# State space output projection: column parts with the norm done part by part, chunks normed six tiles ahead, gates kept in device memory

## The reference, cut to what matters

```python
def _ssd_mixer(h, in_w, conv_w, conv_b, dt_bias, A_log, D_skip, norm_g, out_w):
    ...                                     # z, xs, Bm, Cm, dt from h @ in_w, convolved
    y = _ssd_chunked(xs * dt[..., None], dt * A, Bm, Cm)
    y = y + (xs * D_skip[:, None]).reshape(bsz, L, SSD_D_INNER)
    y = y * jax.nn.silu(z.astype(jnp.float32))
    yg = y.reshape(bsz, L, SSD_N_GROUPS, -1)                       # 8 groups of 512 columns
    yg = yg * lax.rsqrt(jnp.mean(jnp.square(yg), -1, keepdims=True) + RMS_EPS)
    y = yg.reshape(bsz, L, SSD_D_INNER).astype(h.dtype) * norm_g
    return y @ out_w                                               # 256 x 4096 @ 4096 x 2048

x = _layer_norm(DEEPNORM_ALPHA * x + (1.0 + gate) * y, ln_g[layer], ln_b[layer])
if layer == N_A_LAYERS - 1:
    k_sh, v_sh = _shared_kv(x, kv_w)
```

## Time and profile before

| | |
|---|---|
| median of three runs | 3442.06 us |
| profiled execution | 3440.7 us, span 3439.0 us |
| PE busy | 3259.9 us (95%) |
| PEld busy | 2977.3 us (87%) |
| DVE busy | 2384.2 us (69%) |
| ACT busy | 1609.5 us (47%) |
| POOL busy | 677.1 us (20%) |
| chain that ended last | PE 82%, DVE 6%, issue 4%, ACT 3%, PEld 2%, POOL 2%, DMA 1% |
| transfers | 665.63 MB, mean 194 GB/s |

### The profile page before, as it was taken

The page is one execution under the profiler, slowest core; times in us unless marked ns, Lnnn a source line. Parts: engine busy times, 40 slices in busy tenths (PEclk is TensorE's granted clock), DMA queues, the critical chain, the costliest instruction groups (busy, mean ns, idle before and its releaser), DMA issues.

```text
span 3439.0 us, 64842 instructions
## 1 busy us (share of the span) xinstructions
PE 3259.9 (95%) x21994; PEld 2977.3 (87%) x21994; DVE 2384.2 (69%) x3811; ACT 1609.5 (47%) x2252; POOL 677.1 (20%) x636
## 2 busy tenths in 40 slices
PE   7989999999999999999999989999998969999997
PEld 7787899999889998899777879998887859987995
DVE  6665469189778987899898776335777876554455
ACT  4654445533453345433344555445665444444442
POOL 1000029800111001100000116884222111100001
PEclk9999999999999999999999999999999989999998
DMA  6434545666786668766556864656665767765443
GB/s 194 148 98 147 162 147 156 184 203 212 238 264 216 212 219 263 245 209 212 165 172 184 266 210 147 185 188 195 210 207 180 265 210 229 246 192 174 138 129 123
DMA packets 185323, 665.63 MB, mean 194 GB/s; under 512 B 24112, under 2 KB 24320, under 8 KB 184304
## 3 DMA queue, kind: packets, MB, share of 16 engines
q1 hardware_dynamic: 149696, 545.89, 50.0%
q0 software_dynamic: 35504, 118.08, 11.3%
HBM read 661.71 MB, written 2.16 MB: 193 GB/s over the span
## 4 chain that ended last, share of the span: by engine, by line
PE 82%; DVE 6%; issue 4%; ACT 3%; PEld 2%; POOL 2%; DMA 1%; DVEq 0%; SPq 0%; POOLq 0%; PEldq 0%; ACTq 0%
PE PS L564 14%; PE PS L565 14%; PE PS L566 14%; PE PS L914 7%; PE PS L916 6%; PE PS L918 6%; PE PS L635 2%; PE PS L636 2%; PE PS L637 2%; POOL w_lo L465 2%; PE PS L656 2%; PE PS L660 2%; PE PS L658 2%; PE PS L866 1%; ACT w_hi L1259 1%
## 5 line engine op out<-in xcount | busy, mean ns | idle before, releaser
L1259 ACT ACTIVATE w_hi<-raw 128x1024 fp32r<-128x1024 f32 x1032 | 1093.8, 1061 | 1634.5 <-PE PS L566 934.9
L1799 DVE TENSOR_TENSOR w_lo<-raw,w_hi 128x1024 fp32r<-128x1024 f32 x872 | 1072.9, 1233 | 674.1 <-ACT w_hi L1259 668.0
L564 PE MATMUL PS<-xt_hi,w_hi 128*128 128x256 f32 x4608 | 1332.2, 289 | 22.8 <-POOL w_lo L465 7.3
L565 PE MATMUL PS<-xt_lo,w_hi 128*128 128x256 f32 x4608 | 1311.8, 285 | 0.0
L566 PE MATMUL PS<-xt_hi,w_lo 128*128 128x256 f32 x4608 | 1311.1, 285 | 0.0
L564 PEld LDWEIGHTS PS<-xt_hi,w_hi 128*128 128x128 f32 x4608 | 892.5, 194 | 34.6 <-issue 24.2
L565 PEld LDWEIGHTS PS<-xt_lo,w_hi 128*128 128x128 f32 x4608 | 892.6, 194 | 0.4
L566 PEld LDWEIGHTS PS<-xt_hi,w_lo 128*128 128x128 f32 x4608 | 892.0, 194 | 0.0
L465 POOL TENSOR_TENSOR w_lo<-raw,w_hi 128x1024 fp32r<-128x1024 f32 x160 | 405.0, 2540 | 223.0 <-ACT w_hi L1259 222.1
L914 PE MATMUL PS<-w_hi,st_hi 128*128 128x512 f32 x1024 | 403.7, 394 | 1.5 <-issue 1.3
L916 PE MATMUL PS<-w_hi,st_lo 128*128 128x512 f32 x1024 | 400.6, 391 | 0.0
(11 more groups left out here) (381 smaller groups left out, 3571.7 us busy)
## 6 DMA issues: line engine op xcount, KB each, us to landing
raw<-in_u_emb SPq DMA_DIRECT2D x256, 512.0 KB, 3.6
raw<-in_v_emb SPq DMA_DIRECT2D x256, 512.0 KB, 4.3
ada<-in_ada_w POOLq DMA_DIRECT2D x240, 256.0 KB, 4.5
raw<-in_xbc SPq DMA_DIRECT2D x96, 512.0 KB, 3.5
raw<-in_z SPq DMA_DIRECT2D x80, 512.0 KB, 3.6
raw<-in_q SPq DMA_DIRECT2D x64, 512.0 KB, 3.5
raw<-in_a_out SPq DMA_DIRECT2D x64, 512.0 KB, 4.9
raw<-in_k SPq DMA_DIRECT2D x48, 512.0 KB, 4.1
```

Source lines behind the costliest of these rows:

```text
L564: pe.matmul(o, w_h, x_h, start=start, stop=False, skip_group_check=True)
L565: pe.matmul(o, w_h, x_l, start=False, stop=False, skip_group_check=True)
L1259: act.activation(w_hi[:, u, :], raw[:, u, :], ACT.Copy).then_inc(hi_done, 1)
L1799: dve.tensor_tensor(w_lo[:, u, :], raw[:, u, :], w_hi[:, u, :].bitcast(F32), ALU.subtract)\
```

## The change

In the z stage the sums of squares are taken from PSUM by DVE, scaled and inverted at once (`inverted_sum`, at the last head of each group), and ACT takes the root of four groups in one instruction, at head 57 and again at a_out's tile 4. The banks of z and of these sums are other ones.

The projection is unrolled. `norm_tile(i)` does the first 1024 columns of chunk i in tiles 0 to 31 (banks 0 to 3), then 512 columns of two chunks a tile: tiles 32 to 47 into banks 4 and 5, tiles 48 to 63 into banks 6 and 7. The host stores the weights in that order. All chunks keep their high and low parts in `a_hi` and `a_lo`. DVE norms chunk i + 6 and makes the low part of chunk i + 3 at step i. When a part is done, DVE multiplies by the gate row, adds X and takes bn_stats of its columns; parts 0 and 1 do that at steps 33 to 38 and 49 to 54, the last one behind tile 63.

PE transposes the gate (`turn_gates`), ACT copies it, POOL stores it to device memory (`gates_kept`) and reads it back to all partitions as `a_gate` and, before b_out, `gate_row`. The diagonals and their matmuls are gone.

X is normed by mean and root in pieces of 512 columns, half of the tokens on ACT and half on DVE, between the steps of the split that follows PE's transposes. Gain and bias go into that split as scale and bias of each partition (`balanced`, which the xbc stage had before as a written out loop); X itself gets them in `rows_applied`, inside k2 behind its bodies 3 and 6.

```diff
@@ PE
+            def norm_tile(i):
+                pe.wait_ge(lo_done, 4 * FIRST_BODY["a_out"] + i + 1)
+                if i < XC:
+                    pieces = [(i, g * 512, 2 * tt + g, tt) for tt in range(TT) for g in range(2)]
+                else:
+                    part, pair = divmod(i - XC, XC // 2)
+                    pieces = [(2 * pair + k, k * 512, 4 + 2 * part + tt, tt) for k in range(2) for tt in range(TT)]
+                pe.wait_ge(stage_lo_done, CHUNKS["a_out"] + pieces[-1][0] + 1)
...
-            all_rows("a_out", (first_banks, other_banks))
-            gate_rows(0)
-            pe.wait_ge(sem("x4_done"), 1)
+            pe.wait_ge(sem("cb_done"), SG)
+            pe.wait_ge(sem("xd_done"), 2 * SG)
+            pe.wait_ge(sem("sums_out"), SG - 1)
+            for i in range(4 * NB["a_out"]):
+                if i == XC:
+                    pe.wait_ge(sem("z_taken"), XC)
+                    pe.wait_ge(sem("sums_out"), SG)
+                if i == XC + XC // 2:
+                    pe.wait_ge(sem("y_added"), XC)
+                    pe.wait_ge(sem("gates_out"), 1)
+                norm_tile(i)
+                if i == 1:
+                    pe.wait_ge(sem("y_added"), XC - 1)
+                    group_sum(SG - 1, 5)
+                    pe.wait_ge(sem("z_taken"), XC - 1)
+                    ada_sum("z", 3, ada_acc_z)
+                if i == 6:
+                    turn_gates()
             turn(3)
@@ PE, turn
+                    if n == 3 and c % 4 == 0:
+                        pe.wait_ge(sem("x_normed"), c // 4 + 1)
+                        pe.wait_ge(sem("x_normed_too"), c // 4 + 1)
@@ POOL
             pool.wait_ge(sem("sums_out"), SG)
-            pool.wait_ge(sem("gates_split"), 1)
-            norm_operands(0)
-            with pool.Fori(0, 16) as k:
+            ada_tiles("a_out", 0, ada_a)
+            pool.wait_ge(sem("gates_out"), 1)
+            pool.dma_start(gates_kept.rearrange("n (c p) -> c n p", p=P), gate_t[:, :, :]).then_inc(sem("gates_stored"), 16)
+            pool.wait_ge(sem("gates_stored"), 16)
+            pool.dma_start(a_gate[:, :], gates_kept[0].partition_broadcast(P)).then_inc(sem("gate_loaded"), 16)
+            with pool.Fori(1, 16) as k:
                 ada_tiles("a_out", k, ada_a)
-            norm_rows(0)
@@ ACT, a_out
+            for i in range(4 * NB["a_out"]):
+                for c in ((2, 3) if i == 0 else (i + 3,)):
+                    if c < XC:
+                        act.wait_ge(sem("ssd_normed"), c + 1)
+                        act.activation(a_hi[:, c, :], xbc[:, c, :], ACT.Copy).then_inc(stage_hi_done, 1)
+                high(f + 1 + i // 4, i % 4)
+                if i == 4:
+                    act.wait_ge(sem("root_inverted"), SG)
+                    act.activation(rg[:, 4 * S:], rg[:, 4 * S:], ACT.Sqrt).then_inc(sem("group_root"), 1)
+                if i == 7:
+                    act.wait_ge(sem("gates_turned"), 1)
+                    act.activation(gate_t[:, :, :], ...).then_inc(sem("gates_out"), 1)
@@ DVE, z and a_out
+                if k == 7 and g:
+                    inverted_sum(g - 1)
+                if n in (59, 60, 61):
+                    norm_chunk(2 * n - 118)
+                    norm_chunk(2 * n - 117)
...
+            products_at = [int(i >= 4 and i < 62 and i % 6 != 5) for i in range(4 * NB["a_out"])]
+            for i in range(4 * NB["a_out"]):
+                if i + 6 < XC:
+                    norm_chunk(i + 6)
+                for c in ((2, 3) if i == 0 else (i + 3,)):
+                    if c < XC:
+                        chunk_low(c)
+                if i < 63:
+                    low(f + 1 + i // 4, i % 4)
+                if i == 2:
+                    inverted_sum(SG - 1, 5)
+                    modulation_done()
+                if i in part_work:
+                    work, part, tt = part_work[i]
+                    work(part, tt)
+                for _ in range(products_at[i]):
+                    ada_product("a_out", products // 3, products % 3, ada_a, ada_acc_a)
+                    products += 1
...
-            layer_norm(0, "x4_done")
-            turned(3, lambda c: 1.0)
+            balanced(3, pc[:, PC["ln_g"]:PC["ln_g"] + KC], pc[:, PC["ln_b"]:PC["ln_b"] + KC], normed_columns)
+            low(f + 16, 3)
             link(dve.memset(ada_acc_k[:, :, :], 0.0))
...
+            product_bodies("k2", 0, 3, 0)
+            rows_applied(0)
+            product_bodies("k2", 3, 6, 0)
+            rows_applied(1)
+            product_bodies("k2", 6, 12, 0)
+            product_bodies("v2", 0, 4, 12)
```

More of the change, by code:

```diff
@@ L1661, in _ @@
-            f = FIRST_BODY["a_out"]
-            def normed_body(j, group=None):
-                for u in range(4):
-                    high(j + (f + 1), u)
-                    if u % 2 == 1:
-                        if group is not None and u == 1:
-                            act.wait_ge(sem("ssd_normed"), group)
-                        stage("a_out", lambda k: one(xbc, k), 2 * j + (2 + u // 2), u // 2, j + f)
-            with act.Fori(0, SG - 1) as g:
-                normed_body(2 * g)
-                normed_body(2 * g + 1, g + 2)
@@ new lines, in _, with normed_columns @@
+            act.wait_ge(sem("ln_moments"), 1)
+            root(stat[:, 6:8], a_moments[:, :, 1], 1.0, "ln_eps").then_inc(sem("ln_root"), 1)
+            act.wait_ge(sem("ln_scale"), 1)
+            def normed_columns(c):
+                if c in PIECE_AT:
+                    columns = slice(PIECE_AT[c] * 512, PIECE_AT[c] * 512 + 512)
+                    act.activation(X[:, 0, columns], X[:, 0, columns], ACT.Identity, scale=stat[:, 8:9], bias=stat[:, 2:3])\
+                        .then_inc(sem("x_normed"), 1)
@@ L2505, in _ @@
             link(dve.memset(ada_acc_a[:, :, :], 0.0))
             f = FIRST_BODY["a_out"]
-            def normed_body(j, group=None):
-                for u in range(4):
-                    low(j + (f + 1), u)
-                    if u % 2 == 1:
-                        stage(source, 2 * j + (2 + u // 2), u // 2, "a_out")
-                    if u:
-                        ada_product("a_out", j, u - 1, ada_a, ada_acc_a)
-                    if group is not None and u == 1:
-                        norm_group(group)
@@ new lines, in part_added, with part_moments @@
+            def part_added(part, tt):
+                first, n, bank, step = A_PARTS[part]
+                x = X[:, tt, first:first + n]
+                link(dve.scalar_tensor_tensor(x, x, ALPHA, a_product[:, tt, 0:n], ALU.mult, ALU.add))
+            def part_moments(part, tt):
+                first, n, bank, step = A_PARTS[part]
+                for c in range(first // 512, (first + n) // 512):
+                    link.post(dve.bn_stats(a_bn[:, tt, c, :], X[:, tt, c * 512:c * 512 + 512]))
@@ new lines, in _ @@
+            assert products == 48, products
+            for work in (part_product, part_added, part_moments):
+                for tt in range(TT):
+                    work(2, tt)
+            link.wait()
+            for tt in range(TT):
+                last = dve.bn_aggr(a_moments[:, tt, :], a_bn[:, tt, :, :].rearrange("p a b -> p (a b)"))
+                if tt == 0:
+                    link.post(last)
+            last.then_inc(sem("ln_moments"), 1)
+            dve.wait_ge(sem("ln_root"), 1)
@@ L2566, in product_bodies @@
+            def product_bodies(name, start, end, first_k):
+                with dve.Fori(start, end) as j:
                     for u in range(4):
```

427 lines of the change are left out of this document (149 added, 278 removed).

## The result

| | before | after |
|---|---|---|
| median (lowest to highest) | 3441.85 us (3441.38 to 3443.88) | 3421.02 us (3419.37 to 3423.26) |
| profiled execution, span | 3440.7, 3439.0 | 3420.0, 3418.1 |
| ratio, 95% interval | | 0.9941 (0.9928 to 0.9953) |

The kernel is 20.8 us faster, where 24.2 were forecast. The time of 3421 lies 3 above the predicted 3418 and inside the range.

What follows compares the result with a forecast made beforehand. PE sets the time in the long stages, so edits count only where it waits or runs at its low clock. Gains 2.1 + 0.6 + 18.5 + 3.0 = 24.2 us from 3440.7 give 3416.5, plus 1.4 for timed runs 3418; range 3408 to 3430.

Steps and rivals of the forecast that it cites:

- End of z: End of the z stage: reciprocals moved from a_out into z remove PE's waits of 0.82 and 1.80; gain 2.1 us (0 to 3).
- Inside a_out: In the a_out projection: 9.4 us of waits and low clock go, 8.8 new come; gain 0.6 (-6 to 9).
- The wait before tile 0: Start of a_out: PE waits a new 2.7 us for group 6's sum, behind a low half on DVE.
- The round trip: Near a_out's tile 12: loads queue behind the gates' store and read; PE waits about 3 us, plus 1.4 of clock.
- DVE's margin of 0.28 a step: First 26 steps of a_out: DVE needs 2.44 us a step by starts, below PE's 2.72, so it holds.
- (b): a_out: DVE doesn't catch up after the first late load; three more waits of about 2 us, 3424; chance 0.16.
- (d): a_out: DVE becomes the bound of the first 32 tiles, making the kernel slower, 3453; chance 0.04.
- To k2: Last a_out tile to second k2 tile: 23.5 us against 42.0; gain 18.5 (15 to 22).
- rival (e): Before k2: the part norm doesn't shorten the gap, the 18.5 us are lost, 3436; chance 0.05.
- Rival (c): Gap at k2 stays longer, by PE's low clock or bad handovers of column pieces; 10 us more, 3428; chance 0.09.
- k2 and b_out: X's gain and bias cost 0 in k2; gate matmuls and POOL's diagonals leave b_out, gain 3.0 us (1 to 4).
- Rival (a): a_out: round trip short or overtaken by loads, new waits cost no clock; 5.8 us more gain, 3412; chance 0.22.

Runs made afterwards that it cites:

- e5: e1 with the modulation's sum on PE moved from behind a_out's tile 1 to behind tile 4, its use and the gates' turn later too; 3415.07 us.
- e10: e1 with 22 matmuls that add nothing put on PE in its 2.83 us wait before a_out's tile 0; 3411.96 us.
- e12: e10 with more matmuls that add nothing: 50 before the turn of X and 7, 6 and 12 in its waits; 3412.11 us.
- e6: The changed kernel with the first two column parts of a_out normed behind tile 63 together with the last; 3432.67 us.
- e1: The changed kernel with POOL's ada_w loads of steps 1 and 2 issued ahead of the waits for the gates and their store; 3415.15 us.
- e2: The changed kernel with DVE's sum and reciprocal of group 6 moved from the end of head 63 to head 62; 3422.14 us.
- e3: The changed kernel with the edits of e1 and e2 together; 3416.26 us.
- e9: The changed kernel with loads first, the sum of group 6 a head earlier and the modulation's sum behind tile 4 (e3 and e5); 3417.29 us.
- e11: e10 with the modulation's sum moved behind a_out's tile 4, as in e5; 3416.44 us.
- e8: e1 with the modulation's sum behind tile 4 (e5) and the normed columns of X in steps 0 to 3 of the turn; 3415.54 us.
- e4: The kernel before the change, with POOL's product of identity and gates moved behind a_out's loop of loads; 3437.67 us.

## Why the prediction was right, and where its sizes were off

**End of z: right.** 2.1 predicted, 2.1 measured; the waits of 0.82 and 1.80 are gone and the six reciprocals cost nothing. The 0.5 set against them for the root at head 57 came too: it takes 1.06 on ACT instead of 0.51, and PE's wait for `zt` just before 2600 is 1.47 instead of 0.93.

**Inside a_out: waits right, clock too small.** The forecast was a gain of 0.6, the result a loss of 2.3.
- The wait before tile 0: 2.7 predicted, 2.83 measured, from the instruction named. The clock behind it was put at 1.4 and cost 3.0 in after and 1.7 in the other five traces with this wait.
- A second stretch at the lower clock, 1.7, was not foreseen at all. e5 and e10 show it to hang on the wait before tile 0 together with the sparse sum behind it.
- The round trip: 3.0 of wait and 1.4 of clock predicted, 3.17 and 1.5 measured, at tile 12 as said. The 16 KB store of the gates landed in 3.9 us, and in 3.1 to 4.5 over the traces of after and its variants, as the 64 KB store of the earlier trace rows had from another queue (4.1), so a quarter of the bytes made little difference. The 2 us of the Trainium skill's "DMA: Bandwidth & Descriptors" (anatomy of one DMA) for the fixed part are not borne out by this store.
- DVE's margin of 0.28 a step held: no further wait up to tile 63 in after. Rivals (b) and (d) are out.
- These misses add up to 3.7 and the difference is 2.9; where the other 0.8 came back is open.

**To k2: right, 1.2 too good.** 24.7 against 23.5 predicted. The turn starts at 6.3 (6.0), and the second tile ends 18.35 later (17.45). The missing 0.9 is the clock again, as far as the rows tell: the stage that the price of the turn came from had its clock back while it still turned (1.00 in 2050 to 2056), and after's is at 0.60 even in k2's first 4 us. The two rows are of before and of after; e12 shows 2.1 to be had there.

```profile
2050.00:2056.00 6.00, 5.65 (x45) 5.17 (x44) 5.01 (x11) 5.34 (x12) 0.00 (x0) 1.00 0.01 3
```

```profile
2823.20:2827.00 3.80, 3.80 (x22) 3.80 (x21) 3.19 (x8) 3.46 (x8) 0.00 (x0) 0.60 0.00 0
```

e6 puts the part norm's share at 11, and rival (e) is out by that. Rival (c) named this low clock, but at 10 us.

**k2 and b_out: right.** The four 2048-wide instructions cost nothing in k2. The stretch to the end gave 2.9 (3.0), which its spread of 2 us alone would not prove; the 1.23 of waiting and the eight matmuls (1.8) are gone in place.

The term that was mis-sized is thus one, the clock behind short waits: 1.4 for a wait of 2.8 where it was 4.7 in after with both stretches, and 3.3 in e1. Some luck is in the total: 0.9 of the 20.8 comes from the stretch in front that the change doesn't touch, and without it the miss would be 4.3 instead of 3.4. Rival (a), 3412, is what the kernel reaches once the wait at tile 12 is gone and the clock behind the first is held: e10 has 3411.96, with the 2.83 still spent, on filling.

## What to carry to other kernels

Price a wait of TensorE with the clock behind it: here 2.83 us of waiting cost another 3.3 to 4.7 us, 1.6 to 1.7 of it only because a sparse instruction group stood near. If a short wait can't be removed, matmuls that write a bank about to be started afresh can hold the clock. Moving the sparse group alone gained 1.5 in place; taking the wait away by moving one sum (e2, e3) mostly made the next producer late, and so did both moves together (e9). On a queue that issues loads in order, put the loads that are due ahead of a wait for a round trip (e1, 4.7). Treat a reduction part by part as its columns are finished, so that only the last part stands behind the last tile (e6, 10.7).

## What the runs showed of the hardware that was not expected

- A stretch at the 1.2 GHz level can begin some microseconds behind the wait that goes before it, with TensorE busy in between (e11: a wait that ended at 2627.51, the first slow matmuls at 2635.76 to 2638.78).
- 24 one-column matmuls (2.73 us) between full tiles left the clock at the upper level when TensorE had not waited before (e10, e12), and stood in front of a stretch at the lower level when it had, by 0.80 to 2.83 us (after, e2, e11). Three tiles further behind the same wait of 2.83 they left it up (e5, e8).
- Behind one and the same wait of 2.83 us the two tiles took 8.46 us (after) and 7.15 (e1), against 5.44 at the upper level. Behind waits of 3.17, 3.56 and 3.65 at the same tile 7, 14 and 0 matmuls ran at the lower level (after, e2, e6).
- A wait of 0.68 us behind the one-column matmuls was followed by 8 matmuls at the lower level in e4 and by none in the kernel before, whose instructions up to there are the same on TensorE.
